# GpSimd's S5 products put behind its stores of weight sums, and three instructions moved at the head of the second feed-forward

## The chip, the cores and the metric

The kernel runs on one core of one Trainium2 chip. The metric is the device time of one execution in microseconds (us), lower is better. The core's engines are TensorE (PE, with its weight loads as PEld), VectorE (DVE), ScalarE (ACT), GpSimd (POOL) and SyncE (SP, which here only starts transfers). They run side by side, each in its own program order, and wait for one another by semaphores. ACT, POOL and SP can also start DMA transfers.

## The reference

One layer of a decoder trunk in float32, for 512 prompt tokens and 8 x 4 sample tokens (544 columns in all), model width 1024, feed-forward width 2816:

```
h = x + 1/2 * SwiGLU(RMSNorm(x))                                    (macaron half-step FFN 1)
n = RMSNorm(h); P = n @ w_in, with columns split into
    [u_s5 | q | k | v | q_idx | k_idx | w_idx | gate_s5 | gate_att]
branch S5 : complex-diagonal SSM over 32 groups of 16 channels with 64 states per group (ZOH),
            y = Re(C s_t) + D u_t, then GELU and a GLU to D_MODEL
branch DSA: indexer I[t,s] = sum_h w[t,h] relu(q_idx[t,h].k_idx[s]); causal top-k with
            k = min(256, L//4); softmax attention over the GATHERED keys with a T5 relative bias
h = h + (sigmoid(gate_s5) * S5 + sigmoid(gate_att) * DSA) @ w_out
h = h + 1/2 * SwiGLU(RMSNorm(h))                                    (macaron half-step FFN 2)
followed by one final RMSNorm.
```

## The kernel before

**Matrix work.** Activations lie transposed, 128 features on the partitions and the 544 tokens in two halves of 272 columns. Each float32 weight tile is split in two roundings: ACT copies the raw tile (`wraw`) into `w_high`, DVE subtracts to get `w_low`, and PE multiplies high by high, high by low and low by high. So a tile of eight 128 x 128 blocks, called a unit here, is 48 matmuls of 128 x 272.

**First feed-forward** (`ffn1` in each engine's program). The 22 hidden tiles (`FK`) are done in three groups of 8, 8 and 6. A hidden tile takes two units (gate, then up), and after each group there are 8 units of the output product. The order on DVE per hidden tile (`in_tile`): `w_low` of the next two units, gate times up (`sg`), `act_low`. SP loads the raw tiles, four slots deep.

**Weight sums.** In the first feed-forward DVE has time to spare, and uses it for the second one, which is computed with 7 products a tile instead of 8 from sums of weight blocks. For each of the 22 columns of weights `c`, GpSimd loads four pieces (`sum_loads`, 4 x 256 KB) into a buffer (`sums_even`, or `sums_odd` together with `ohs`, by the parity of `c`), DVE adds them in place (`weight_sums`, four instructions), and GpSimd stores them to memory (`sum_stores`, 4 x 256 KB to `scr_w`). `sum_loads(c)` waits until the stores of `c - 2` have landed, since it writes the same buffer. On GpSimd the loads of `c + 1` stand ahead of the stores of `c`, all in one program order. On DVE `weight_sums` is written into the sequence by hand: one after a hidden tile from the third tile of group 1 on and in group 2, and one after each second unit of an output product (`k % 2`) of the groups 1 and 2.

**S5 products.** GpSimd also forms 9 `lag_product`s and 8 `step_product`s for the S5 branch, six small instructions each (L2016 four times, L2019, L2020). Eight of the lag products stand inside the loop over `c`, two each at `c` = 18 to 21, between `sum_loads(c + 1)` and `sum_stores(c)`. After the last one `prep_done` lets PE turn the S5 input matrices (L1018).

**Head of the second feed-forward.** PE comes out of the `w_out` product (8 units, L814) and goes over to the 7-product tiles (L908). Product `p` of the first tile takes its right-hand blocks as they become ready (`first_blocks`): block `j` needs DVE's addition to `hT`, ACT's `scaled` and `block_high`, DVE's `cross_sums`, ACT's `cross_high`, DVE's `cross_low`. `first_out` (L1546) is ACT's copy of the bank of product 0 into `mid`, which PE needs before product 4, as that goes into the same bank. `combine` on DVE takes `mid` and two banks and frees the bank that product 5 needs.

## Time and profile before

| what | value |
|---|---|
| time, median of 3 runs | 1432.33 us (1430.95 to 1442.85) |
| the profiled execution's own time | 1438.22 us |
| its span | 1436.6 us |
| PE busy | 1349.9 us (94%) |
| PEld busy | 1263.0 us (88%) |
| DVE busy | 815.6 us (57%) |
| ACT busy | 541.1 us (38%) |
| POOL busy | 380.8 us (27%) |
| PE's share of the chain that ended last | 81% |
| mean granted TensorE clock | 0.973 |

"Busy" is the time in which an engine ran instructions. The chain that ended last is followed back from the last instruction, at each step to what released it. The span is what lies between the first and the last instruction of the profiled execution.

### The profile page before, as it was taken

What the parts mean: (1) busy time and instruction counts of PE and PEld (TensorE: products, weight loads), DVE (VectorE), ACT (ScalarE), POOL (GpSimd) and SP (SyncE); (2) the same over time, 40 slices, a digit from 0 to 9 for tenths busy, and PEclk for the clock granted to TensorE, in tenths of its full rate; (3) what the DMA queues carried; (4) which work ended last, traced back from release to release, by engine and by line L of the source; (5) the groups of instructions that cost most, each with busy time, mean ns of one, the idle gap of its engine ahead of it and who ended that gap; (6) DMA issues with size and microseconds to landing.
All of it is one profiled execution on the core that took longest, in us unless ns stands there. A gap on an engine that the chain in (4) does not pass through costs nothing.

```text
span 1436.6 us, 28358 instructions
## 1 busy us (share of the span) xinstructions
PE 1349.9 (94%) x11158; PEld 1263.0 (88%) x11158; DVE 815.6 (57%) x1381; ACT 541.1 (38%) x801; POOL 380.8 (27%) x501
## 2 busy tenths in 40 slices
PE   6999999997999898997999989899989999999996
PEld 5999999997996777885899977669989999999996
DVE  4355555663544223993898631416688747764864
ACT  5433222211234031124678632332564414432544
POOL 4144434488923300221457632210000000000000
PEclk9999999998999899998999989999999999999998
DMA  9678778865334363335222387864445425533431
GB/s 132 198 243 255 254 238 269 263 177 175 91 101 101 59 101 94 79 102 72 66 60 60 84 290 254 297 213 145 133 133 175 145 80 180 178 115 117 141 89 63
DMA packets 244672, 216.25 MB, mean 151 GB/s; under 512 B 32001, under 2 KB 203145, under 8 KB 244570
## 3 DMA queue, kind: packets, MB, share of 16 engines
q1 hardware_dynamic: 202272, 138.38, 32.9%
q0 software_dynamic: 21808, 66.12, 15.5%
q10 hardware_dynamic: 20490, 10.36, 3.4%
q8 instruction: 67, 1.10, 0.3%
q14 instruction: 35, 0.29, 0.1%
HBM read 182.22 MB, written 31.41 MB: 149 GB/s over the span
## 4 chain that ended last, share of the span: by engine, by line
PE 81%; DVE 5%; DMA 4%; ACT 3%; issue 3%; POOL 2%; SPq 1%; ACTq 0%; DVEq 0%; POOLq 0%
PE ps L814 25%; PE ps L908 15%; PE ps L792 9%; PE ps L958 9%; PE ps L1267 4%; PE ps L1283 3%; PE ps L1384 3%; PE ps L1353 2%; DMA wraw<-in_w_ffn_in 2%; PE ps L1436 1%; DVE uv L2615 1%; PE ps L1050 1%; PE ps L1415 1%; POOL kvtok L2016 1%; PE ps L1298 1%
## 5 line engine op out<-in xcount | busy, mean ns | idle before, releaser
L2130 DVE TENSOR_TENSOR w_low<-wraw,w_high 128x1024 fp32r<-128x1024 f32 (+1 forms) x121 | 150.1, 1242 | 145.4 <-ACT w_high L1500 129.7
L1500 ACT ACTIVATE w_high<-wraw 128x1024 fp32r<-128x1024 f32 x75 | 79.4, 1060 | 248.8 <-PE ps L814 241.2
L814 PE MATMUL ps<-hn_high,w_high 128*128 128x272 f32 x704 | 147.6, 291 | 12.9 <-DVE w_low L2130 12.9
L814 PE MATMUL ps<-hn_high,w_low 128*128 128x272 f32 x704 | 147.0, 291 | 0.0
L814 PE MATMUL ps<-hn_low,w_high 128*128 128x272 f32 x704 | 146.8, 290 | 0.0
L814 PEld LDWEIGHTS ps<-hn_high,w_high 128*128 128x128 f32 x704 | 112.3, 191 | 13.4 <-issue 13.4
L814 PEld LDWEIGHTS ps<-hn_low,w_high 128*128 128x128 f32 x704 | 112.3, 191 | 0.0
L814 PEld LDWEIGHTS ps<-hn_high,w_low 128*128 128x128 f32 x704 | 111.4, 191 | 0.0
L814 PE MATMUL ps<-act_high,w_high 128*128 128x272 f32 x464 | 96.5, 289 | 1.9 <-DVE sg L2130 1.1
L814 PE MATMUL ps<-act_high,w_low 128*128 128x272 f32 x464 | 96.0, 288 | 0.0
L814 PE MATMUL ps<-act_low,w_high 128*128 128x272 f32 x464 | 95.7, 287 | 0.0
L814 PEld LDWEIGHTS ps<-act_high,w_high 128*128 128x128 f32 x464 | 72.7, 188 | 2.7 <-DVE sg L2130 1.4
L958 PE MATMUL ps<-act_high,w_high 128*128 128x272 f32 x352 | 73.3, 289 | 0.0
L958 PE MATMUL ps<-act_high,w_low 128*128 128x272 f32 x352 | 72.9, 288 | 0.0
L814 PEld LDWEIGHTS ps<-act_low,w_high 128*128 128x128 f32 x464 | 72.8, 188 | 0.0
L958 PE MATMUL ps<-act_low,w_high 128*128 128x272 f32 x352 | 72.6, 288 | 0.0
L814 PEld LDWEIGHTS ps<-act_high,w_low 128*128 128x128 f32 x464 | 72.4, 189 | 0.0
L792 PE MATMUL ps<-wslot,hn 128*128 128x256 f32 (+2 forms) x336 | 68.4, 369 | 2.8 <-ACT kvtok L1759 2.0
L792 PEld LDWEIGHTS ps<-wslot,hn 128*128 128x128 f32 (+1 forms) x336 | 59.2, 199 | 10.7 <-issue 2.6
L792 PE MATMUL ps<-hn,wslot 128*128 128x272 f32 (+1 forms) x272 | 65.0, 401 | 2.3 <-DMA wslot<-in_w_in 2.3
L792 PEld LDWEIGHTS ps<-hn,wslot 128*128 128x128 f32 (+1 forms) x272 | 51.3, 194 | 16.4 <-DMA wslot<-in_w_in 3.2
L908 PE MATMUL ps<-xc_high,w_high 128*128 128x272 f32 x352 | 58.6, 288 | 1.3 <-ACT xc_high L1526 1.3
(442 smaller groups left out, 3096.6 us busy)
## 6 DMA issues: line engine op xcount, KB each, us to landing
wraw<-in_w_ffn_in SPq DMA_DIRECT2D x44, 512.0 KB, 5.0
wraw<-in_w_ffn_out SPq DMA_DIRECT2D x32, 512.0 KB, 4.4
sums_even<-in_w_ffn_in POOLq DMA_DIRECT2D x44, 256.0 KB, 4.0
scr_w<-sums_even POOLq DMA_DIRECT2D x44, 256.0 KB, 3.5
wfront<-scr_w SPq DMA_DIRECT2D x44, 256.0 KB, 3.5
wraw<-scr_w SPq DMA_DIRECT2D x44, 256.0 KB, 3.5
wfront<-in_w_ffn_in SPq DMA_DIRECT2D x33, 256.0 KB, 3.4
wraw<-in_w_ffn_in SPq DMA_DIRECT2D x33, 256.0 KB, 3.2
```

What stands on the lines that cost most here:

```text
L792: ins = pe.matmul(dst, a, b, start=(k == 0), stop=(k == len(pairs) - 1), **kw)
L814: ins = pe.matmul(ps[:, bank + h, 0:HALF], a[:, k, :], x[:, lo_at(k) if x is x_lo else k, h * HALF:(h + 1) * HALF], start=(k == 0 and a is ...
L908: ins = pe.matmul(bank_of(f, p), a[:, k, :], x[:, XC[p], k, :], start=(n == 0 and k == 0 and p < 4), stop=(n == order[2] and k == 3), skip ...
L958: ins = pe.matmul(ps[:, 4 * (j % 2) + h, 0:HALF], a[:, k, :], side(x[:, k, :], h), start=(k == 0 and n == 0), stop=(k == m - 1 and n == 2) ...
L1050: pe.matmul(ps[:, b + m, :], w[:, k, P * m:P * m + P], hn[:, k, 0:SEQ], start=(k == 0), stop=(k == DK - 1))
L1267: ins = pe.matmul(ps[:, 4 * slot + h, 0:HALF], w[slot][:, P * k:P * k + P], act[:, k, cols_h], start=(m == 0), stop=(m == 3 * DK - 1), ski ...
L1283: ins = pe.matmul(ps[:, 4 * o + part, 0:HALF], w[:, (4 * o + k) * P:(4 * o + k + 1) * P], g_k, start=(p == 0 and k == 0), stop=(p == 2 and ...
L1298: pe.matmul(ps[:, 2 + 5 * o, 0:w], qT[r, x % 8 // 2, P * qb:P * qb + P], kT[r, x % 8 // 2, 0:w], start=True, stop=True).then_inc(s["scores ...
L1353: ins = pe.transpose(ps[:, 3 + j, P * c:P * c + P], kpage[i % 4][c][:, P * j:P * j + P], ident[:])
L1384: ins = pe.matmul(ps[:, 7, 0:HALF], w[:, k, :], act[:, k, h * HALF:(h + 1) * HALF], start=(p == 0 and k == 0), stop=(p == 2 and k == DK - ...
L1500: act_e.activation(wh[:, j % 2, :, :], wraw[:, j, :, :], ACT.Copy).then_inc(s["hi_done"], 1)
L2130: return dve.tensor_tensor(o, a, b, op)
```

## The change

Five edits, none of which changes what is computed:

1. GpSimd's first `sum_loads` wait for the fourth unit of PE instead of the second.
2. In GpSimd's loop `sum_stores(c)` comes ahead of the S5 products, and the products are one a round at `c` = 17 to 21 instead of two a round at 18 to 21; four lag products (5 to 8) instead of one follow the loop.
3. On DVE each `weight_sums` stands one place later: the first after the fourth hidden tile, the last (column 21) after the first tile of the third group.
4. At the end of the `w_out` product: ACT's rounding of the first tile's first pieces (`tile_high_pair(0, 0, 0)`) goes behind `square(2, 6)` and `cross_high(6)`; DVE's `add_square(2, 6)` goes from before the addition to `hT` of block 7 to behind `cross_sums(7)`.
5. ACT's `first_out(0, 1)` goes from behind the first tile's `silu2` and `hidden_high` to ahead of that `silu2`.

```
@@ GpSimd
-            pool.wait_ge(s["unit_done"], 2)
+            pool.wait_ge(s["unit_done"], 4)
...
             for c in range(FK):
                 if c < FK - 1:
                     sum_loads(c + 1)
-                if c == FK - 4:
+                sum_stores(c)
+                if c == FK - 5:
                     pool.wait_ge(s["s5_scalars"], 2)
                     pool.wait_ge(s["early_act"], 1)
-                if c >= FK - 4:
-                    for k in range(2):
-                        lag_product(2 * (c - FK + 4) + k, 2 * (c - FK + 4) + k)
-                sum_stores(c)
-            lag_product(8, 8)
+                if c >= FK - 5:
+                    lag_product(c - FK + 5, c - FK + 5)
+            for k in range(5, 9):
+                lag_product(k, k)
             for k in range(CH):
                 step_product(k, 9 + k)
@@ VectorE, first feed-forward
-                                    if f0 == 8 or (f0 == 0 and lo):
-                                        weight_sums(2 * lo + j + (10 if f0 else -2))
+                                    if 3 <= f0 + 2 * lo + j <= 16:
+                                        weight_sums(2 * lo + j + {0: -3, 8: 9, 16: 21}[f0])
...
                             if k % 2:
-                                weight_sums((18 if f0 else 6) + k // 2)
+                                weight_sums((17 if f0 else 5) + k // 2)
@@ ScalarE, end of the w_out product
                 block_high(j)
-                if j == 6:
-                    tile_high_pair(0, 0, 0)
                 square(2, j)
                 cross_high(j)
                 if j == 6:
+                    tile_high_pair(0, 0, 0)
                     tile_high_pair(0, 0, 1)
@@ VectorE, end of the w_out product
                     cross_low(6)
                     tile_low_pair(0, 0, 0)
+                else:
                     add_square(2, 6)
-                else:
                     add_square(2, 7)
@@ ScalarE, ffn2
-                        first_out(g, f)
+                        if f != 1:
+                            first_out(g, f)
...
                             for q in (1, 2):
                                 tile_high_pair(g, f + 1, q)
+                            if f == 0:
+                                first_out(0, 1)
                             silu2(f)
                             tile_high_pair(g, f + 1, 3)
```

**GpSimd, from the last round without a product on.** `scr_w<-` are the stores of weight sums, `<-in_w_ffn_in` the loads of pieces, and one S5 product is a row of four multiplications and two rows that write `biasmem`. Before:

```order
L2009 DMA scr_w<-ohs 128x512 x2
L2003 DMA sums_odd<-in_w_ffn_in 128x4x128 x2
L2003 DMA ohs<-in_w_ffn_in 128x4x128 x2
L2016 ISA
L2016 TENSOR_TENSOR kvtok<-qkT,kis 128x256 x4
L2019 TENSOR_TENSOR biasmem<-kvtok 128x16x16
L2020 TENSOR_TENSOR biasmem<-kvtok 128x16x16
L2016 TENSOR_TENSOR kvtok<-qkT,kis 128x256 x4
L2019 TENSOR_TENSOR biasmem<-kvtok 128x16x16
L2020 TENSOR_TENSOR biasmem<-kvtok 128x16x16
L2009 DMA scr_w<-sums_even 128x512 x4
L2003 DMA sums_even<-in_w_ffn_in 128x4x128 x4
```

Now:

```order
L2011 DMA scr_w<-sums_odd 128x512 x2
L2011 DMA scr_w<-ohs 128x512 x2
L2018 ISA
L2018 TENSOR_TENSOR kvtok<-qkT,kis 128x256 x4
L2021 TENSOR_TENSOR biasmem<-kvtok 128x16x16
L2022 TENSOR_TENSOR biasmem<-kvtok 128x16x16
L2005 DMA sums_odd<-in_w_ffn_in 128x4x128 x2
L2005 DMA ohs<-in_w_ffn_in 128x4x128 x2
L2011 DMA scr_w<-sums_even 128x512 x4
L2018 TENSOR_TENSOR kvtok<-qkT,kis 128x256 x4
L2021 TENSOR_TENSOR biasmem<-kvtok 128x16x16
L2022 TENSOR_TENSOR biasmem<-kvtok 128x16x16
```

Two products stood between a load and the next store; now one product stands between a store and the next load.

**DVE, from the last unit but one of group 2's output product into the third group.** `hT<-ps,hT` closes a unit, `w_low` prepares the next ones. Before:

```order
L2319 SCALAR_TENSOR_TENSOR hT<-ps,hT 128x544
L2130 TENSOR_TENSOR w_low<-wraw,w_high 128x1024
L2130 TENSOR_TENSOR sums_odd<-sums_odd 128x512
L2130 TENSOR_TENSOR sums_odd<-sums_odd,ohs 128x512
L2130 TENSOR_TENSOR ohs<-ohs,sums_odd 128x512
L2130 TENSOR_TENSOR ohs<-ohs 128x512
L2326 UNCONDITIONAL_BRANCH
L2130 TENSOR_TENSOR w_low<-wraw,w_high 128x1024 x2
L2130 TENSOR_TENSOR sg<-sg,ps 128x544
L2130 TENSOR_TENSOR act_low<-sg,act_high 128x544
```

Now:

```order
L2321 SCALAR_TENSOR_TENSOR hT<-ps,hT 128x544
L2132 TENSOR_TENSOR w_low<-wraw,w_high 128x1024
L2132 TENSOR_TENSOR sums_even<-sums_even 128x512 x4
L2328 UNCONDITIONAL_BRANCH
L2132 TENSOR_TENSOR w_low<-wraw,w_high 128x1024 x2
L2132 TENSOR_TENSOR sg<-sg,ps 128x544
L2132 TENSOR_TENSOR act_low<-sg,act_high 128x544
L2132 TENSOR_TENSOR sums_odd<-sums_odd 128x512
L2132 TENSOR_TENSOR sums_odd<-sums_odd,ohs 128x512
L2132 TENSOR_TENSOR ohs<-ohs,sums_odd 128x512
L2132 TENSOR_TENSOR ohs<-ohs 128x512
```

The sums of column 21 (`sums_odd` and `ohs`) stood ahead of the two `w_low` of the third group; now those of column 20 stand there, and column 21 follows `act_low` of the group's first tile.

**ACT, first tile of the second feed-forward.** `mid<-ps` is `first_out`, `sg<-sg` is `silu2`, `act_high` is `hidden_high`. Before:

```order
L1486 ACTIVATE rstd<-ps,epsc 128x544
L1537 ACTIVATE w_high<-wraw 128x1024
L1537 ACTIVATE more_high<-wraw 128x1024
L1550 ACT_TABLE_LOAD
L1550 ACTIVATE sg<-sg 128x544
L1537 ACTIVATE more_high<-wraw 128x512
L1554 ACTIVATE act_high<-sg 128x544
L1546 ACTIVATE mid<-ps 128x272
```

Now:

```order
L1486 ACTIVATE rstd<-ps,epsc 128x544
L1537 ACTIVATE w_high<-wraw 128x1024
L1537 ACTIVATE more_high<-wraw 128x1024
L1546 ACTIVATE mid<-ps 128x272
L1550 ACT_TABLE_LOAD
L1550 ACTIVATE sg<-sg 128x544
L1537 ACTIVATE more_high<-wraw 128x512
L1554 ACTIVATE act_high<-sg 128x544
```

The copy `mid<-ps` now stands ahead of the table load and the activation, where it stood behind both and behind `act_high`.

## Rows read from the trace of the kernel before

**Rows 1.** Waits of PE, 20 to 443 us: total us, times, longest.
```profile
PE ps L814 <- DVE w_low L2130: 12.9, 3, 8.3
```

**Rows 2.** Timeline of PE, 322 to 350 us: start us, us, instruction, [idle before, releaser].
```profile
334.87 0.41 PE L814 MATMUL ps<-hn_high,w_low 128*128 128x272 f32 x2
343.55 0.82 PE L814 MATMUL ps<-hn_high,w_high 128*128 128x272 f32 x2 [8.27 <-DVE w_low L2130]
```

**Rows 3.** Windows around it: us, busy (instructions) by engine, PEclk, DMA share, GB/s.
```profile
344.00:350.00 6.00, 6.00 (x32) 6.00 (x32) 4.19 (x3) 0.66 (x1) 5.61 (x10) 0.60 0.85 266
350.00:360.00 10.00, 10.00 (x82) 10.00 (x81) 1.84 (x2) 2.64 (x3) 9.53 (x15) 1.00 0.56 191
```

**Rows 4.** Timeline of DVE, 275 to 350 us.
```profile
324.39 1.23 DVE L2130 TENSOR_TENSOR w_low<-wraw,w_high 128x1024 fp32r<-128x1024 f32 x1 [0.37 <-ACT w_high L1500]
337.51 1.15 DVE L2130 TENSOR_TENSOR sums_odd<-sums_odd 128x512 f32<-128x512 f32 x1 [11.90 <-DMA ohs<-in_w_ffn_in]
...
341.67 3.42 DVE L2130 TENSOR_TENSOR w_low<-wraw,w_high 128x1024 fp32r<-128x1024 f32 x2
```

**Rows 5.** Timeline of POOL, 262 to 425 us.
```profile
311.50 3.37 POOL L2016 TENSOR_TENSOR kvtok<-qkT,kis 128x256 f32<-128x256 f32 x4
...
323.16 1.15 POOL L2009 DMA_DIRECT2D scr_w<-sums_odd  x2 [0.30 <-POOL biasmem L2020]
...
330.57 1.51 POOL L2003 DMA_DIRECT2D sums_odd<-in_w_ffn_in  x2 [5.21 <-DMA scr_w<-ohs]
```

**Rows 6.** The chain that ended last, 300 to 350 us: start us, us, what.
```profile
324.83 5.17 DMA scr_w<-ohs
...
332.81 4.68 DMA ohs<-in_w_ffn_in
```

**Rows 7.** Timeline of POOL, 24 to 70 us.
```profile
38.39 3.03 POOL L2003 DMA_DIRECT2D sums_even<-in_w_ffn_in  x4 [11.16 <-PE ps L814]
```

**Rows 8.** Timeline of PE, 49 to 53 us.
```profile
51.85 0.49 PE L814 MATMUL ps<-hn_high,w_high 128*128 128x272 f32 x2 [1.74 <-DVE w_low L2130]
```

**Rows 9.** The chain that ended last, 20 to 60 us.
```profile
24.00 25.27 DMA wraw<-in_w_ffn_in
```

**Rows 10.** Timeline of DVE in the third group, 346 to 414 us.
```profile
346.44 2.47 DVE L2130 TENSOR_TENSOR act_low<-sg,act_high 128x544 fp32r<-128x544 f32 x1 [0.72 <-ACT act_high L1644]
...
386.49 1.10 DVE L2130 TENSOR_TENSOR act_low<-sg,act_high 128x544 fp32r<-128x544 f32 x1 [0.73 <-ACT act_high L1644]
...
407.49 1.23 DVE L2130 TENSOR_TENSOR w_low<-wraw,w_high 128x1024 fp32r<-128x1024 f32 x1 [4.59 <-ACT w_high L1500]
...
410.07 0.73 DVE L2130 TENSOR_TENSOR act_low<-sg,act_high 128x544 fp32r<-128x544 f32 x1 [0.72 <-ACT act_high L1644]
```

**Rows 11.** Timeline of PE, 409 to 411 us.
```profile
410.85 0.52 PE L814 MATMUL ps<-act_high,w_high 128*128 128x272 f32 x2 [0.80 <-DVE act_low L2130]
```

**Rows 12.** Timeline of POOL: the S5 products behind the last stores.
```profile
358.37 3.35 POOL L2016 TENSOR_TENSOR kvtok<-qkT,kis 128x256 f32<-128x256 f32 x4
...
401.78 1.72 POOL L2020 TENSOR_TENSOR kvtok<-kvtok 128x256 f32<-128x256 f32 x1
```

**Rows 13.** Timeline of PE: the first use of the S5 products.
```profile
448.62 3.62 PE L1018 MATMUL ps<-ident_sb,kvtok 128*128 128x128 f32 x20
```

**Rows 14.** Timeline of PE, 1036 to 1092 us, head of the second feed-forward.
```profile
1052.06 0.39 PE L908 MATMUL ps<-xc_high,w_high 128*128 128x272 f32 x1 [1.34 <-ACT xc_high L1526]
...
1068.65 0.99 PE L908 MATMUL ps<-xc_high,more_high 128*128 128x272 f32 x4 [2.20 <-ACT mid L1546]
...
1071.69 1.10 PE L908 MATMUL ps<-xc_high,more_high 128*128 128x272 f32 x4 [0.23 <-DVE mid L2130]
...
1075.14 0.66 PE L908 MATMUL ps<-xc_high,w_high 128*128 128x272 f32 x4
```

**Rows 15.** Timeline of DVE, same stretch (this one is `add_square(2, 6)`).
```profile
1047.43 0.72 DVE L2130 TENSOR_TENSOR rstd<-rstd,sg 128x544 f32<-128x544 f32 x1
```

**Rows 16.** Windows at that place.
```profile
1070.00:1072.00 2.00, 1.77 (x8) 1.45 (x8) 1.86 (x4) 0.49 (x1) 0.00 (x0) 0.50 0.45 128
```

## The prediction
> **What bounds the kernel now.** I read the page first: PE is busy 94% of the span and makes 81% of the chain that ended last. So a change on GpSimd, DVE and ACT can only give back time in which PE stood still or ran at the lower of its two clocks, and I went through the waits of PE, then the timelines of the engines it waited for, then the chain.
>
> In the first feed-forward PE waits for `w_low` 12.9 us in three waits [rows 1]. The longest, 8.27 us, ends at 343.55 [rows 2]. It is DVE's: the next `w_low` was due at about 330, but DVE had finished the one at 324.39 and then stood 11.90 us before `sums_odd`, for a transfer [rows 4]. That transfer's history is GpSimd's program order: from 311.50 two S5 products, the stores of column 19 only at 323.16 behind the second one, 5.17 us until they landed, the loads of column 21 at 330.57, 4.68 us until the last piece landed at 337.49 [rows 5, 6]. After the wait PE runs at a granted clock of 0.60 in the mean (it was at the lower of its two clocks, 1.2 GHz, until about 348.6) and issues 32 matmuls in 6 us, where ten full-speed microseconds hold 82 [rows 3].
>
> A second wait is 1.74 us before the unit at 51.85 [rows 8]: the raw weights of that unit were asked for at 24.00 and landed after 25.27 us [rows 9], and from 38.39 on GpSimd put 1 MB of first pieces beside them [rows 7]. The third, at the very first unit, is not touched.
>
> At the head of the second feed-forward PE waits 1.34 us for the last `cross_high`, 2.20 us for `first_out` of the second tile, 0.23 us for `combine` [rows 14], and the clock after it is 0.50 [rows 16].
>
> **Stores ahead of the products, sums one place later.** On DVE the place where 21 stood (behind 324.39) now holds 20, and 21 comes after the group's first `act_low`, some 12 us further on. On GpSimd, stores of 19 now follow at once the sums of 19, in the place of the old column 20 (before 319.4). With 2.2 us of issue and the 5.17 us of [rows 6] they are down by about 324; the product between them and the next load ends there too, since one takes (403.5 - 358.37) / 9 = 5.0 us [rows 12]. Column 20, one round before, is loaded about 12 us earlier, so by 321 at the latest, and 21 by about 332, where it is wanted at about 340. The 11.90 us of DVE go, and with them PE's **8.3 us**. The lower clock cost, from 344 to 350, 6 x 8.2 - 32 = 17 matmuls of 0.122 us, 2.1 us, and half of the 0.45 us before: **2.3 us**. What is late next there is nothing of this chain: the four sums of 21 cost DVE about 2.7 us in a tile that has 12 us of PE work, as they did in every tile of group 2 without a wait of PE.
>
> **First pieces later.** The first 1 MB leaves GpSimd at about 50 instead of 38.39. The raw loads then have their engines to themselves between 38 and 49. Nothing in the trace shows them alone. Lower bound: no gain, if the parameter loads before 38 are what holds them. Upper: the whole **1.7 us**, since ACT and DVE need some 2.5 us from landing to PE, so landing by 47.5 is enough, 1.8 us earlier than now, and 1 MB at the 260 GB/s of the first feed-forward takes 4 us. I take 1.7: the needed part is less than half of what is moved away. The first sums are used near 80, so their lateness is covered by 20 us.
>
> **Products that run longer.** Four products more stand behind the last stores: 13 in place of 9, so from about 345 to 345 + 13 x 5.0 = 410 instead of 403.5, in a program that is 12 us ahead by then. Two things lie under them. One is the wait of 0.80 us at 410.85 [rows 11], where PE needs the last `act_low` of the third group, behind a `w_low` and a `sg`. GpSimd was quiet then. With it busy, DVE took 1.10 and once 2.47 us for `act_low` instead of 0.73 [rows 10], and 1.7 for `w_low` instead of 1.23 [rows 4, 10]. So this wait grows by 0.4 + 0.5, less where they don't meet: I take **-0.8 us**, bounds 0 and -2.4. The other is `prep_done`, wanted at 448.62 [rows 13], now about 437; 410 leaves 27 us.
>
> The Trainium skill speaks against the change at this place (GPSIMD Engine Reference, Key points): GpSimd shares its SBUF interfaces with VectorE and contends with DVE instructions of two SBUF inputs. Of that kind are `w_low`, `act_low` and the sums. The rows agree in direction, but PE hides it everywhere except in this one chain: by the rule the sum is the one below, without it 0.8 us more.
>
> **Head of the second feed-forward.** DVE's `add_square(2, 6)` at 1047.43 takes 0.72 us [rows 15] and stood ahead of the last addition to `hT`, which could have begun at 1046.85; `w_low` before it ends later than that too, because ACT rounded those weights before `cross_high(6)`. With both moved, that addition comes about 1.2 us earlier, and so does the last `cross_high`; its wait shrinks from 1.34 to about 0.4. All that follows is about 1.0 us earlier; the moved `add_square` then takes some of it back ahead of `cross_low(7)`, 0.2 us at most.
>
> `first_out(0, 1)`: what it waits for, product 0 of the second tile, ends some 5 us before `silu2` can run. So it costs ACT nothing and the 2.20 us vanish. But the next thing late is DVE's `combine` of the second tile, at 1071.69 [rows 14], which hangs on the first tile's `gate2` and `hidden_low` and on two `w_low`, not on this copy. Product 4 runs early, and PE then waits before product 5 instead: about 3.8 us in one piece. From the end of `combine` PE has what it had. The slow 1071.69 to 1075.14 (3.45 us for 24 matmuls, 0.43 over full speed) can become 3.0 or, as one long idle stretch ends at the lower clock, 4.6. So the head gives 1.0 + 0.43, less 0 to 1.6: **+0.6 us**, bounds -0.2 and +1.4.
>
> **Sum.** 8.3 + 2.3 + 1.7 - 0.8 + 0.6 = 12.1 us. The profiled execution took 1438.22 us, so it would take 1426.1. It stands 5.9 us above the median of the runs, 1432.33; taking the same gain off the median gives **1420.2 us**.
>
> **The rivals.**
> *The ordinary run has less of this stall.* The two waits of the chain for stores and loads are transfers, and landing times vary; the profiled execution is 5.9 us above the median, and this stall is the one part of it that hangs on several transfers in a row. If all 5.9 us are here, the gain is 12.1 - 5.9 = 6.2 and the median 1426.1. Against it: products and issue alone account for most of the chain and are the same in each run. Chance 0.2.
> *The pieces are late again.* One product between stores and loads may last longer, and DVE would wait at 20 instead of 21. The margin worked out above is 4 to 5 us, beyond which DVE's lateness reaches PE after another 3.7 us. If half the stall stays, with the clock, the gain is about 6.8 and the time 1425.5. Chance 0.07.
> *More than the sum.* With all terms at their upper bound the gain is 8.3 + 2.3 + 1.7 - 0 + 1.4 = 13.7; stretches at the lower clock elsewhere, which shift with the start of each, could add a few us: 1416. Chance 0.15.
> *Slower: the S5 products become the bound.* PE stands before L1018 until the 17th product. It decides when 13 products end after 437, that is above (437 - 345) / 13 = 7.1 us each; the kernel is slower than before by over 1% only above (437 + 12.1 + 14.3 - 345) / 13 = 9.1 us each, at 1447. The rows give 5.0. Chance 0.03.
> The forecast itself has 0.55; its own range, from the bounds of its terms, is 1417 to 1425.
>
> **How the numbers follow.** One per cent is 14.3 us, about what a measurement of this kernel can tell from no change. The forecast and the first two rivals lie within it; of the third about two thirds and of the forecast a small part lie beyond it. Faster by over 1%: 0.18. Slower by over 1%: 0.03. Within: 0.79. The range takes in the first two rivals and most of the third: 1415 to 1428.
>
> **What would show it right or wrong.** Right: no wait of DVE for a piece above 1 us after 280; no PE wait near 330 and full clock there; PE's wait near 50 gone; the wait at the third group's end at 1 to 2 us; at the second feed-forward's head no wait for `mid` from ACT, and one of 3 to 4 us for `mid` from DVE. Wrong: PE waiting for `w_low` after any of the sums of 18 to 21, the raw load of the third tile still landing near 49, L1018 waiting for POOL, or a lower-clock stretch of over 4 us at the head.

## The result, and the profile after

| what | before | after |
|---|---|---|
| time, median | 1435.51 us (1430.95 to 1442.85, 8 runs) | 1424.24 us (1419.81 to 1433.99, 8 runs) |
| ratio of the two, 95% interval | | 0.9934 (0.9909 to 0.9959) |
| the profiled execution's own time | 1438.22 us | 1423.19 us |
| its span | 1436.6 us | 1421.5 us |
| mean granted TensorE clock | 0.973 | 0.974 |

The forecast was 1420.2 us in a range of 1415 to 1428, and no change beyond 1% as the likeliest case. The medians are 11.3 us apart, and the ratio says 0.66% less, 9.5 us (0.41% to 0.91%). The time lies inside the range, 4 us above the forecast, and the change is within 1% as forecast.

The page of the kernel after, its busy times:

```profile
span 1421.5 us, 28355 instructions
PE 1344.5 (95%) x11158; PEld 1257.4 (88%) x11158; DVE 814.3 (57%) x1381; ACT 541.6 (38%) x801; POOL 380.2 (27%) x501
```

The longest waits of PE from 20 to 440 us (total us, times, longest), which answer to [rows 1]. The second of them is at L802, which before reaches only behind the window of [rows 1]: there it waits for the same `rstd`, for 2.28 us too.

```profile
PE ps L814 <- DVE w_low L2132: 2.9, 1, 2.9
PE ps L802 <- DVE rstd L2132: 2.3, 1, 2.3
PE ps L814 <- DVE act_low L2132: 0.9, 1, 0.9
```

Of the three waits for `w_low` only the very first is left. I cut both executions at the same places of the program and compare the pieces:

| stretch | before | after | gained |
|---|---|---|---|
| start of the span to the first L814 | 24.07 | 23.69 | 0.4 |
| first feed-forward, to L802 behind it | 421.64 | 410.16 | 11.5 |
| middle (projections, S5, DSA, `w_out`), to the first L908 | 600.95 | 596.24 | 4.7 |
| head: first L908 to the third tile's first product | 28.48 | 29.86 | -1.4 |
| rest | 361.46 | 361.55 | -0.1 |

The first feed-forward gave the sum of its terms (8.3 + 2.3 + 1.7 - 0.8 = 11.5), to the digit only by luck: two of the terms were off in opposite directions, as told further down. The head lost where a gain was forecast. The middle is a matter of its own, since the only edited instructions in it are those at its end that edit 4 swaps. In the 14 profiled executions of this case it took 590.2 to 604.0 us, and most of that lies between L1065 and L1267 (191.4 to 201.1 us), where the granted clock differs from 0.92 to 0.97. The windows of that stretch, rounded to whole us (width, then busy time and instructions of PE, PEld, DVE, ACT, POOL, then clock, DMA share, GB/s), first for the execution of experiment e6, then for that of e12, with the same code there:

```profile
495.00:696.00 201.00, 182.48 (x1518) 145.23 (x1517) 105.62 (x340) 54.06 (x116) 27.20 (x30) 0.92 0.41 85
```

```profile
475.00:667.00 192.00, 174.60 (x1519) 140.45 (x1520) 105.93 (x344) 53.97 (x116) 27.21 (x30) 0.97 0.44 89
```

So a single profiled span tells no gain of less than some 10 us, and the 15.1 us between the two spans above are 4.7 us too flattering. Gains of a stage are read between landmarks of that stage, and their value for the whole from medians.

### The profile page after: what moved, and what is told of

Same layout as the page of the kernel before. It is cut to its first block, busy times and chain, and to the rows that moved or that the text cites. A ratio compares the mean times of both kernels' runs of the same rounds, so it can differ in the third digit from the quotient of the medians.

```text
span 1421.5 us, 28355 instructions
## 1 busy us (share of the span) xinstructions
PE 1344.5 (95%) x11158; PEld 1257.4 (88%) x11158; DVE 814.3 (57%) x1381; ACT 541.6 (38%) x801; POOL 380.2 (27%) x501
## 4 chain that ended last, share of the span: by engine, by line
PE 88%; DVE 4%; ACT 3%; issue 2%; DMA 1%; SPq 1%; ACTq 0%; DVEq 0%
PE ps L814 31%; PE ps L908 16%; PE ps L792 9%; PE ps L958 9%; PE ps L1267 4%; PE ps L1283 3%; PE ps L1384 3%; PE ps L1353 2%; PE ps L1436 1%; DVE uv L2617 1%; PE ps L1415 1%; PE ps L1050 1%; PE ps L1298 1%; PE ps L1157 1%; PE ps L1307 1%
## 5 line engine op out<-in xcount | busy, mean ns | idle before, releaser
L814 PE MATMUL ps<-hn_high,w_high 128*128 128x272 f32 x704 | 146.8, 290 | 2.9 <-DVE w_low L2132 2.9
L814 PE MATMUL ps<-hn_high,w_low 128*128 128x272 f32 x704 | 146.7, 290 | 0.0
L814 PE MATMUL ps<-hn_low,w_high 128*128 128x272 f32 x704 | 146.1, 289 | 0.0
L814 PEld LDWEIGHTS ps<-hn_high,w_high 128*128 128x128 f32 x704 | 111.9, 190 | 3.0 <-issue 3.0
L814 PEld LDWEIGHTS ps<-hn_low,w_high 128*128 128x128 f32 x704 | 111.6, 190 | 0.0
L814 PEld LDWEIGHTS ps<-hn_high,w_low 128*128 128x128 f32 x704 | 110.9, 191 | 0.0
L814 PE MATMUL ps<-act_high,w_high 128*128 128x272 f32 x464 | 96.6, 289 | 2.2 <-DVE sg L2132 1.1
L814 PE MATMUL ps<-act_high,w_low 128*128 128x272 f32 x464 | 96.0, 288 | 0.0
L814 PE MATMUL ps<-act_low,w_high 128*128 128x272 f32 x464 | 95.7, 287 | 0.0
L814 PEld LDWEIGHTS ps<-act_high,w_high 128*128 128x128 f32 x464 | 72.7, 188 | 3.1 <-DVE sg L2132 1.4
L814 PEld LDWEIGHTS ps<-act_low,w_high 128*128 128x128 f32 x464 | 72.8, 188 | 0.0
L814 PEld LDWEIGHTS ps<-act_high,w_low 128*128 128x128 f32 x464 | 72.4, 189 | 0.0
L908 PE MATMUL ps<-xc_high,w_high 128*128 128x272 f32 x352 | 58.8, 289 | 0.7 <-ACT xc_high L1526 0.7
```

What stands on the lines that cost most here:

```text
L814: ins = pe.matmul(ps[:, bank + h, 0:HALF], a[:, k, :], x[:, lo_at(k) if x is x_lo else k, h * HALF:(h + 1) * HALF], start=(k == 0 and a is ...
L908: ins = pe.matmul(bank_of(f, p), a[:, k, :], x[:, XC[p], k, :], start=(n == 0 and k == 0 and p < 4), stop=(n == order[2] and k == 3), skip ...
```

## What the trace of after shows at the places of the prediction

**The stall.** Timeline of DVE, the four sums that end the second group (start us, us, instruction, [idle before, releaser]), against [rows 4]:

```profile
302.27 3.13 DVE L2132 TENSOR_TENSOR sums_even<-sums_even 128x512 f32<-128x512 f32 x4 [1.92 <-DMA sums_even<-in_w_ffn_in]
...
315.30 0.69 DVE L2132 TENSOR_TENSOR sums_odd<-sums_odd 128x512 f32<-128x512 f32 x1 [2.38 <-DMA ohs<-in_w_ffn_in]
...
327.17 3.36 DVE L2132 TENSOR_TENSOR sums_even<-sums_even 128x512 f32<-128x512 f32 x4 [2.71 <-DMA sums_even<-in_w_ffn_in]
330.44 1.22 DVE L2132 TENSOR_TENSOR w_low<-wraw,w_high 128x1024 fp32r<-128x1024 f32 x1
...
339.67 0.69 DVE L2132 TENSOR_TENSOR sums_odd<-sums_odd 128x512 f32<-128x512 f32 x1 [0.38 <-DMA ohs<-in_w_ffn_in]
```

The 11.90 us are gone, but DVE still waits for pieces before four sums, up to 2.71 us. GpSimd's timeline over the same stretch, against [rows 5], shows why:

```profile
308.99 2.18 POOL L2011 DMA_DIRECT2D scr_w<-sums_even  x4
311.19 3.37 POOL L2018 TENSOR_TENSOR kvtok<-qkT,kis 128x256 f32<-128x256 f32 x4
314.63 0.76 POOL L2021 TENSOR_TENSOR biasmem<-kvtok 128x256 f32<-128x256 f32 x1
315.34 1.26 POOL L2022 TENSOR_TENSOR biasmem<-kvtok 128x256 f32<-128x256 f32 x1
318.38 3.04 POOL L2005 DMA_DIRECT2D sums_even<-in_w_ffn_in  x4 [1.78 <-DMA scr_w<-sums_even]
321.41 1.11 POOL L2011 DMA_DIRECT2D scr_w<-sums_odd  x2
```

The stores come first, then one product. It ends at 316.60, but the loads leave only at 318.38, because they wait for the stores in front of the product, which landed some 7 us behind the end of their issue at 311.17. The four sums for which the loads are wanted start at 327.17, when the last piece has landed, 8.8 us after the first load was issued. PE nevertheless has no wait. The lateness of 2.71 us is less than what DVE is ahead of PE there: before, 11.90 us of waiting on DVE made 8.27 us on PE [rows 2, 4], which leaves some 3.6 us. The window over the whole place, where before had a clock of 0.60 in the mean for 6 us [rows 3]:

```profile
320.00:350.00 30.00, 30.00 (x242) 30.00 (x241) 17.93 (x18) 7.32 (x9) 24.86 (x35) 1.00 0.83 261
```

**The head of the second feed-forward.** Timeline of PE, against [rows 14]:

```profile
1034.30 0.39 PE L908 MATMUL ps<-xc_high,w_high 128*128 128x272 f32 x1 [0.66 <-ACT xc_high L1526]
...
1054.35 1.27 PE L908 MATMUL ps<-xc_high,more_high 128*128 128x272 f32 x4 [3.72 <-DVE mid L2132]
...
1059.05 1.11 PE L908 MATMUL ps<-xc_high,more_low 128*128 128x272 f32 x4
1059.95 0.85 PE L908 MATMUL ps<-xc_high,w_high 128*128 128x272 f32 x4
```

and the window behind the wait:

```profile
1053.00:1060.00 7.00, 5.65 (x25) 5.65 (x26) 4.07 (x8) 1.60 (x2) 0.00 (x0) 0.54 0.66 187
```

The wait for `first_out` has become one wait of 3.72 us for `combine`, as forecast. The 24 matmuls behind it, 1054.35 to 1059.95, took 5.60 us where the profiled execution of before had 3.45 and full speed is 3.0: the clock was at the lower of its two levels to the end of both products. The experiments on the head show how far this is the edit's doing.

## The experiments

Times are medians. Each ratio is against the kernel before, measured in the same set on the same chip (1433.98, 1432.17 and 1434.20 us over 21, 31 and 30 runs for e1 to e4, e5 to e8 and e9 to e12). The three sets ran on three chips, so times of different sets are compared by their ratios. The ratio is not exactly that of the two medians.

| run | kernel | time, us | ratio, 95% interval | FFN 1 | middle | head |
|---|---|---|---|---|---|---|
| e1 | after without edit 5 | 1422.08 | 0.992 (0.9895 to 0.9945) | 409.8 | 602.8 | 27.38 |
| e2 | after, `combine` earlier | 1420.53 | 0.9917 (0.9884 to 0.995) | 409.5 | 597.9 | 23.39 |
| e3 | before + edits 2, 3 | 1426.12 | 0.9946 (0.9927 to 0.9964) | 409.9 | 593.1 | 28.28 |
| e4 | before + edit 5 | 1435.98 | 1.0017 (0.9997 to 1.0036) | 421.5 | 596.6 | 29.67 |
| e5 | before + edit 2 | 1424.68 | 0.9937 (0.9909 to 0.9965) | 414.6 | 596.2 | 28.47 |
| e6 | before + edit 3 | 1443.45 | 1.0061 (1.0032 to 1.0089) | 429.6 | 604.0 | 30.49 |
| e7 | before + edit 1 | 1431.23 | 0.9977 (0.9952 to 1.0002) | 420.1 | 593.8 | 30.31 |
| e8 | after without edit 1 | 1424.30 | 0.9935 (0.9911 to 0.9959) | 410.0 | 601.1 | 29.87 |
| e9 | before + edit 5, `combine` earlier | 1430.79 | 0.9974 (0.9949 to 0.9998) | 420.5 | 597.3 | 24.16 |
| e10 | before + edit 4 | 1433.73 | 1.0005 (0.998 to 1.0029) | 419.8 | 600.0 | 27.39 |
| e11 | after, once more | 1424.00 | 0.9935 (0.9915 to 0.9955) | 409.1 | 595.6 | 29.78 |
| e12 | e2, once more | 1421.98 | 0.9922 (0.9892 to 0.9952) | 410.1 | 590.2 | 23.39 |

### Which edits make the gain: e3, e5, e6

e3 is before with GpSimd's and DVE's parts of the main edit, and nothing else:

```
+                sum_stores(c)
+                if c >= FK - 5:
+                    lag_product(c - FK + 5, c - FK + 5)
...
+                                    if 3 <= f0 + 2 * lo + j <= 16:
+                                        weight_sums(2 * lo + j + {0: -3, 8: 9, 16: 21}[f0])
```

> The kernel before with the second and third edit alone (stores ahead of products, sums one place later). Theory A: the 8.3 us wait of PE near 335 and the slow stretch behind it go, the wait of 1.7 us near 51 stays, the head of the second feed-forward is as before: the end of the first feed-forward comes 10 us earlier than in the profile of before, the kernel about 10 us faster, 0.993. Theory B (part of the gain of the whole change came from elsewhere than its profile shows): under 6 us.

Its first feed-forward takes 409.9 us, as in after, and its ratio of 0.9946 holds four fifths of the gain of 0.9934, with overlapping intervals. So the stall and the clock behind it are most of the gain. The wait of 1.7 us near 51, which was expected to stay, was not there in this execution.

e5 has GpSimd's part alone (`sum_stores(c)` ahead of the products, one product a round), e6 has DVE's part alone (each `weight_sums` one place later).

> The kernel before with the second edit alone (stores ahead of products, one product a round from column 17 on); DVE's sums stand where they stood. Theory A (the order on GpSimd is all of the stall): the stores of column 19 follow its sums at about 305, its loads of 21 go out at about 312 and are down by 320, before DVE wants them at 326: PE's wait of 8.3 us and the slow stretch go, the first feed-forward ends 10 us earlier, the kernel is at 0.993. Theory B (the later place of the sums is what gives room): DVE still waits some us before column 21 and PE 1 to 5 us, and the kernel gains under 7 us.

> The kernel before with the third edit alone (each weight sum one place later), the two products a round still between loads and stores. Theory A: the stall moves with the sums and keeps its size: two products still delay the stores of 19 to about 335 and the pieces of 21 to about 350, DVE waits some 10 us before them behind the first act_low of the third group, PE about 8 us near 347, then the lower clock; the kernel is as before within 2 us. Theory B (12 us more room are enough): no wait of PE above 1 us, 10 us gained.

e5 is as fast as both together (0.9937 against 0.9946), though its first feed-forward ended 7.0 us earlier than that of before and not 10. e6 is not neutral, it is 0.6% slower than before (0.3 to 0.9%), 9 to 11 us. Its waits of PE from 20 to 450 us, and DVE's two sums, from its timeline:

```profile
PE ps L814 <- DVE w_low L2130: 18.1, 4, 9.1
```

```profile
334.17 3.77 DVE L2130 TENSOR_TENSOR sums_even<-sums_even 128x512 f32<-128x512 f32 x4 [9.03 <-DMA sums_even<-in_w_ffn_in]
...
356.79 0.90 DVE L2130 TENSOR_TENSOR sums_odd<-sums_odd 128x512 f32<-128x512 f32 x1 [13.54 <-DMA ohs<-in_w_ffn_in]
```

and GpSimd's side of it:

```profile
330.42 2.36 POOL L2016 TENSOR_TENSOR kvtok<-qkT,kis 128x256 f32<-128x256 f32 x4
...
340.04 1.72 POOL L2020 TENSOR_TENSOR biasmem<-kvtok 128x256 f32<-128x256 f32 x1
342.06 1.15 POOL L2009 DMA_DIRECT2D scr_w<-sums_odd  x2 [0.30 <-POOL biasmem L2020]
...
350.30 1.51 POOL L2003 DMA_DIRECT2D sums_odd<-in_w_ffn_in  x2 [6.03 <-DMA scr_w<-ohs]
```

A sum that comes later on DVE makes its stores later, and with two products still between sums and stores the whole chain slips by more than the place gained. The direction I expected, a stall that moves with the chain, was there; its size was not. Column 20 now stalls too, and the one stall has become two, 4.83 and 9.09 us of PE. So edit 3 has no worth of its own. Edit 2 removes the cause.

On top of edit 2, edit 3 makes the pieces later too. In e5 DVE starts the sums of columns 20 and 21 without any wait:

```profile
316.42 2.62 DVE L2130 TENSOR_TENSOR sums_even<-sums_even 128x512 f32<-128x512 f32 x4
...
328.44 0.68 DVE L2130 TENSOR_TENSOR sums_odd<-sums_odd 128x512 f32<-128x512 f32 x1
```

With edits 2 and 3 it waits for the pieces of column 20 in each of seven executions (after, e1, e2, e3, e8, e11, e12), from 1.91 to 4.05 us. A sum that is later on DVE has later stores, and these hold back the loads of the column after next. PE pays nothing for it in any of them, but the lateness that after still shows comes with edit 3.

Whether edit 3 gains anything else on top of edit 2 is open. In the trace of e5 PE has a new wait that e3 has not, 2.99 us at 288.36 for a `w_low`. DVE's timeline of e5 and then GpSimd's:

```profile
282.67 3.20 DVE L2130 TENSOR_TENSOR qkT<-qkT,ident_sb 16x512 f32<-16x512 f32 x1 [0.15 <-DVE qkT L2130]
285.90 0.72 DVE L2319 SCALAR_TENSOR_TENSOR hT<-ps,hT 128x544 f32<-128x544 f32 x1
286.54 1.68 DVE L2130 TENSOR_TENSOR w_low<-wraw,w_high 128x1024 fp32r<-128x1024 f32 x1
```

```profile
282.94 2.37 POOL L2016 TENSOR_TENSOR kvtok<-qkT,kis 128x256 f32<-128x256 f32 x4
```

and the same DVE instruction in e3, where GpSimd's first product comes only after 296 us:

```profile
282.24 0.68 DVE L2130 TENSOR_TENSOR qkT<-qkT,ident_sb 16x512 f32<-16x512 f32 x1 [0.15 <-DVE qkT L2130]
```

A DVE instruction that reads two SBUF operands took 3.20 us instead of 0.68 while a GpSimd product ran beside it, and `w_low` behind it came late. In all 13 other executions it took 0.68 us, and no product ran beside it. The Trainium skill says that GpSimd shares its SBUF interfaces with VectorE and contends with DVE instructions of two SBUF inputs (GPSIMD Engine Reference, Key points); the pair of rows agrees. In this trace the first feed-forward is 4.7 us longer than with both edits, but the ratios of e5 and e3 show nothing of it. Whether the collision happens in every execution of e5 wasn't tried.

### The first pieces: e7, e8

e7 is before with this one line, e8 is after with it undone:

```
-            pool.wait_ge(s["unit_done"], 2)
+            pool.wait_ge(s["unit_done"], 4)
```

> The kernel before with the first edit alone (first pieces asked for after the fourth unit). Theory A (the pieces take the raw loads' bandwidth): the raw load issued at about 24 lands by 47.5 and PE's wait near 50 is gone, 1.7 us gained, not distinguishable by time; the 8.3 us near 335 stay. Theory B (that load is late or not by chance of each execution, whatever the pieces do): the landing stays at 48 to 50, or differs as much between kernels that have the pieces at the same place.

> The changed kernel with its first edit undone (first pieces after the second unit). Theory A (the pieces take the raw loads' bandwidth): PE waits 1 to 3 us near 50 again, the first feed-forward is that much longer, the rest as in the changed kernel; by time not distinguishable from it. Theory B (chance of each execution): a landing anywhere between 44 and 50, as e3 with the pieces at the same place had no wait there and e4 had 2.7 us.

The wait of PE behind the raw load of the third tile, with first pieces at the second unit: 1.74, 0, 2.77, 0.31, 1.33, 0.37, 0 and 0 us in before, e3, e4, e5, e6, e8, e9 and e10, a mean of 0.8. With first pieces at the fourth unit it is 0 in each of after, e1, e2, e7, e11 and e12. The 0.37 us of e8 is less than the 1 to 3 us expected. The chain that ended last in e8 still holds the load, landing at 47.73:

```profile
24.04 23.69 DMA wraw<-in_w_ffn_in
```

while in after it has no transfer between 20 and 60 us:

```profile
23.69 36.43 PE ps L814 x268
```

ACT starts on that tile at 45.0 to 46.8 us in the six executions with the edit and at 46.9 to 49.3 in the eight without. The two groups do not overlap, so the cause is as forecast, and the 1.7 us of the profiled execution are one draw from 0 to 2.8. The times (e8 at 0.9935 against 0.9934 of after, e7 at 0.9977 with an interval up to 1.0002) can't tell 0.8 us from nothing.

### The head: e1, e4, e10, e2, e9, and e11 with e12

e4 is before with edit 5 alone, and e1 is after with the same lines taken back:

```
-                        first_out(g, f)
+                        if f != 1:
+                            first_out(g, f)
...
+                            if f == 0:
+                                first_out(0, 1)
```

e10 is before with edit 4 alone, which moves `tile_high_pair(0, 0, 0)` behind `cross_high(6)` on ACT and `add_square(2, 6)` behind `cross_sums(7)` on DVE.

> The changed kernel with its fifth edit undone: the copy first_out(0, 1) stands behind the second feed-forward's first silu2 and hidden_high again. Theory A (the long idle stretch costs): PE waits twice, about 2.2 and 0.2 us, instead of once 3.7 us; the clock is low for less of the work behind; from the first L908 to the third tile's first product it takes about 28.0 us, 1.8 less than the 29.86 us of the changed kernel's profile; the whole is 0 to 2 us faster than the changed kernel. Theory B (the long slow stretch was chance of one profile): the stretch takes as long as in the changed kernel, within 0.5 us, and so does the kernel.

> The kernel before with the fifth edit alone (first_out(0, 1) early). Theory A: PE's waits of 2.2 and 0.2 us at the head become one of about 3.8 us before product 5, the time of that stretch rises by 0.5 to 2.2 us through the lower clock, nothing else moves: the kernel is 0 to 2 us slower, not distinguishable by time. Theory B (the copy was what PE waited for): the head is 2 us shorter.

> Before with edit 4 alone (order at the end of the w_out product). Theory A (as predicted): PE's wait for the last xc_high falls from 1.34 to about 0.4 to 0.7 us and the head, first to third tile, takes 27.4 us instead of 28.5; median 1 us under before's, not to be told from it. Rival B (the delayed rounding of the first tile's weights makes w_low the late one): a wait of PE for w_low or xc_low of over 1 us appears there and the median is 0 to 2 us above before's.

The timeline of PE in e10:

```profile
1047.54 0.39 PE L908 MATMUL ps<-xc_high,w_high 128*128 128x272 f32 x1 [0.66 <-ACT xc_high L1526]
...
1064.56 0.77 PE L908 MATMUL ps<-xc_high,more_high 128*128 128x272 f32 x4 [2.20 <-ACT mid L1546]
...
1067.60 0.77 PE L908 MATMUL ps<-xc_high,more_high 128*128 128x272 f32 x4 [1.26 <-DVE mid L2129]
```

and in e4:

```profile
1066.30 0.77 PE L908 MATMUL ps<-xc_high,more_high 128*128 128x272 f32 x4 [3.72 <-DVE mid L2133]
...
1068.32 1.11 PE L908 MATMUL ps<-xc_high,more_high 128*128 128x272 f32 x4
```

Two numbers separate the edits: the time from the first L908 until `combine` lets product 5 start, and that of the 24 matmuls that follow.

| | executions | to the start of product 5 | the 24 matmuls | head |
|---|---|---|---|---|
| head as before | before, e3, e5, e6, e7 | 25.03 to 25.04 | 3.45, 3.25, 3.43, 5.45, 5.27 | 28.48, 28.28, 28.47, 30.49, 30.31 |
| edit 4 | e10, e1 | 24.27, 24.26 | 3.12, 3.12 | 27.39, 27.38 |
| edit 5 | e4 | 25.03 | 4.64 | 29.67 |
| edits 4 and 5 | after, e8, e11 | 24.26, 24.27, 24.27 | 5.60, 5.60, 5.51 | 29.86, 29.87, 29.78 |

Edit 4 makes product 5 start 0.77 us earlier. Edit 5 moves it by nothing, because `combine` hangs on other things, and only collects PE's idle time into one wait of 3.72 us.

What the 24 matmuls take is a matter of the clock, and it varies with the head unchanged. In before, e3 and e5 the clock fell early, about 22 us into the head, and was back up some 26 us into it, so that most of the slow stretch lay ahead of product 5, where PE would have waited anyway. In e6 and e7, with the same code of the head, it fell later and stayed down through nearly all of both products. PE's timeline in e6 and the window behind:

```profile
1078.70 0.77 PE L908 MATMUL ps<-xc_high,more_high 128*128 128x272 f32 x4 [2.20 <-ACT mid L1546]
...
1081.74 1.27 PE L908 MATMUL ps<-xc_high,more_high 128*128 128x272 f32 x4 [1.09 <-DVE mid L2130]
```

```profile
1082.00:1087.00 5.00, 5.00 (x23) 5.00 (x24) 2.60 (x5) 1.60 (x2) 0.00 (x0) 0.50 0.67 214
```

Idle time in two pieces of 2.20 and 1.09 us was thus followed by 5.45 us for the 24 matmuls in e6, and in two pieces of 2.20 and 1.26 us by 3.12 us in e10. So the two pieces do not by themselves keep the clock up. Edit 5 alone (29.67 us) lies inside the 28.28 to 30.49 of the heads without it, and no loss is shown. On top of edit 4 the three heads with edit 5 are 2.4 to 2.5 us longer than the two without, but whether edit 4 alone always keeps the clock up is not shown by two executions. e4 at 1.0017 (0.9997 to 1.0036) and e1 at 0.992 against 0.9934 of after lean to a loss by edit 5, without being told from zero. What is shown is that edit 5 gains nothing.

The remedy that follows is to make `combine` itself early. e2 is after, and e9 is before with edit 5, with this on DVE:

```
                         if f > f0:
                             combine_up0(g, f - 1)
+                            if f == 1:
+                                dve.wait_ge(s["combined"], combined_at(0, "up0"))
+                                combine(g, f)
                             gate2(f - 1)
+                            if f == 1:
+                                dve.wait_ge(s["ffn_ev"], gated_at(0))
+                                combine_up1(g, f)
...
-                        if f:
+                        if f > 1:
                             combine(g, f)
                             combine_up1(g, f)
```

> The changed kernel, and DVE's combine of the second tile of the second feed-forward is put ahead of the first tile's gate2, its combine_up1 right behind that gate2. Theory A (at the head PE waits for DVE's combine alone, and everything else has slack): the wait of 3.7 us before product 5 falls to under 0.3 us, the clock stays at the higher level, the head takes 3.7 + 2.6 = about 6 us less, the kernel about 1418 where the changed one takes 1424. Theory B (the next thing is late at once: w_low of the first tile's last pair or of the third tile): a wait of 1 to 3 us comes back at product 6 or at the third tile, and at most 3 us are gained.

> Before with the early copy (edit 5) and, on DVE, the second tile's combine ahead of the first tile's gate2; the first feed-forward as before. Theory A (the early copy pays nothing by itself because DVE's combine is late next and PE then has one idle stretch of 3.7 us with half the clock behind it; with combine moved as well both are gone): the head, from the first to the third tile's first product, falls from 28.5 to about 24 us (a little more than the 23.4 it took when the last cross_high also came earlier), no wait above 1 us in it but the 1.3 us at the last cross_high, clock 1.00; the median 4 to 5 us under before's. Rival B (the 23.4 us came from edit 4 or from a more favourable clock in that execution): head 27 to 30 us, median within 2 us of before's.

> The changed kernel itself, so that its time is measured on the same chip and against the same runs of before as the next one. Both theories: 1421 to 1425 us; a profile with the FFN 1 stretch at 410 us and the head at 29 to 30 us.

> The changed kernel with DVE's combine of the second tile ahead of the first tile's gate2, a second time beside the changed kernel. Theory A (the 6 us that its head was shorter are in every execution): head 23 to 24 us again, median 4 to 6 us under that of the changed kernel in this same set. Rival B (the middle of the kernel, which varies by 10 us from execution to execution, made the earlier difference): head as before or median within 2 us of the changed kernel.

The waits of PE in e12 from 1020 to 1090 us, and the window over its head:

```profile
PE ps L908 <- DVE mid L2132: 0.9, 1, 0.9
PE ps L908 <- ACT xc_high L1526: 0.7, 1, 0.7
PE ps L908 <- DVE xc_low L2132: 0.2, 1, 0.2
```

```profile
1028.00:1052.00 24.00, 23.27 (x180) 22.90 (x181) 22.42 (x32) 14.94 (x21) 0.00 (x0) 1.00 0.49 155
```

The head takes 23.39 us in both executions of this kernel, 6.4 less than in after, and the clock stays full. In e9, on top of before, it is 24.16, against 28.28 to 30.49 with the head as before, so the gain hangs neither on edit 4 nor on a lucky execution. Part of it is paid back in the third tile, where a new wait of 0.94 us for `mid` stands: the rest of the span is 362.6 us in e2 and e9 and 363.3 in e12, against 361.5. Some 4.6 to 5.4 us should stay. The medians show less: e12 is 2.0 us below e11 in the same set, where 4 to 6 were expected, and e9 is 3.4 us below before, where 4 to 5 were. Pooled over chips, the kernel has a mean of 1420.7 us (13 runs, standard error 1.4) and after 1425.0 us (20 runs, 0.8): 4.3 us less, with an interval of 1.1 to 7.5. e9 against e4, on two chips, is 1430.6 against 1435.5 in the mean (12 runs each), 4.8 us less. So the shorter head is shown by the traces, and its size in the whole time only roughly. At 0.992 of before this is the fastest version I found together with e1, from which its time does not tell it.

## Why the prediction was right, and where not

**What bounds, and the stall: right.** The 8.3 us of [rows 2] went, PE's waits show nothing in their place, and e5 shows that GpSimd's program order was the cause, by itself. The clock term of 2.3 us was somewhat large: 11.5 us gained less 8.27 + 1.74 for the two waits, plus 0.15 for the grown one, leave 1.6 for the clock and for all else. The 0.7 us too much here and the 0.65 us too much charged for the S5 products, below, cancel, which is luck. Other executions say much the same as this pair: the mean of the first feed-forward is 420.8 us in four without edits 1 to 3 (before, e4, e9, e10) and 409.7 us in five with them (after, e1, e2, e11, e12).

**"Loaded by 321 at the latest", "no wait of DVE for a piece above 1 us": wrong.** The pieces landed at 327.2, and DVE waited 1.92, 2.38 and 2.71 us. The sum had the stores down 5.17 us behind their issue, by the end of the product between, and the last piece landing 4.68 us behind the issue of its load, as in [rows 6]. In after the stores took some 7 us to land, the loads left at 318.38, their issue alone took 3.04 us, and the last piece was there 8.8 us after the first issue. The pieces of column 21, forecast for 332, were there at 339.7. By e5, where DVE has no such wait, part of the lateness comes from edit 3, in which the prediction saw only room. It cost PE nothing, but the margin that I gave as 4 to 5 us was about 1 us in this execution. e8, where DVE waited 4.05 us and PE not at all, shows that there is a little more. The rival with late pieces was nearer than its 0.07.

**First pieces later: right in kind.** 1.7 us in the profiled execution, 0.8 in the mean of eight.

**S5 products: right.** They end at 410, as worked out, 27 us before L1018 at 436.97. The loss of 0.8 us under them was too large: the wait for the third group's last `act_low` grew from 0.80 [rows 11] to 0.95 us in after, to 1.3 or 1.4 us in e2, e3, e6 and e8. The engines met less often than I charged.

**Head: the waits right, the clock wrong.** That `combine` is late next, and that PE has 3.7 us idle in one piece, stood in the prediction and in the trace. The first term was 0.77 us where I had 1.0. The step that failed is the clock: "can become 3.0 or, as one long idle stretch ends at the lower clock, 4.6". It became 5.51 to 5.60 us with edits 4 and 5, 4.64 in e4. That bound lets half the clock last 3.2 us; it lasted through both products. The term was -1.4 us instead of +0.6, outside its bounds of -0.2 and +1.4. The 3.45 us that the sum took from were no fixed cost either: the same head took 3.25 to 5.45 us for these matmuls in five executions, and against their mean head of 29.2 us the loss is 0.6 us. One of the prediction's own signs of being wrong, a stretch of over 4 us at the lower clock at the head, did come.

**The median: 4 us off.** The head is 2.0 us of it, profile against profile. The rest fits the number from which I took the gain: 1432.33 was the median of three runs. Over larger sets before has 1432.2 to 1435.5, with 1434.2 over the 30 runs of the last. 1434.2 - 12.1 + 2.0 is 1424.1, and after was measured at 1424.2 and 1424.0. From the two ends of that range the same sum gives 1422.1 and 1425.4, so the close agreement is partly the choice of that number. The forecast's own range is also a little wide at one end: the upper bounds of the terms give 13.7 us and thus 1418.6, not 1417. The rival of a stall that is smaller in ordinary runs needed a profiled execution that is slow because of it. But PE's stall is much the same in every execution with GpSimd's and DVE's old order: 8.3 us in before and 7.9, 7.3, 8.1 and 8.0 us in e4, e7, e9 and e10. The 5.9 us over the median fit the middle, 601.0 us against a mean of 597.5 over the 14 executions, and the small sample.

## What to carry to other kernels

Where one in-order queue carries both the stores that free a buffer and work with no hurry, put the stores first and spread the rest over the rounds. To move the consumer later instead makes such a loop slower. When a wait is removed, ask what is late next: if that holds the engine until the same instant as before, the edit gains nothing and only gathers idle time into one piece. Before a loss or gain of 2 us behind a wait is put down to an edit, look at the same place in other executions with unchanged code, since the clock there can differ by as much. Compare profiled executions stage by stage between landmarks, and never take a gain from two spans whose untouched part varies by more than the gain.

## What the runs showed of the hardware that I had not expected

- Idle time of TensorE in two pieces, with a product between, was followed by the full clock in e1 and e10 (2.20 and 1.26 us, then 24 matmuls in 3.12 us) and by the lower one in e6 and e7 (2.20 and 1.09, 2.20 and 0.78 us, then 5.45 and 5.27 us). One piece of 3.72 us was followed by 5.5 to 5.6 us for those matmuls in after, e8 and e11, and by 4.64 in e4. What decides between them stays open.
- One DVE instruction took 3.20 us beside a GpSimd product (e5), and 0.68 us in the 13 executions in which none ran beside it.
- With the same code the middle of the kernel took 590.2 to 604.0 us, at a granted clock of 0.92 to 0.97 in its most variable stretch. What decides that clock from one execution to the next stays open.
